# A chunked state-space scan: skip term per head, differences by one-scalar pieces, one exponential per group, the state's decay on two engines

## The reference

```python
acs = jnp.cumsum(dt * A, axis=2)                       # per chunk, always <= 0 and falling
seg = acs[:, :, :, None] - acs[:, :, None, :]
Lmat = jnp.exp(jnp.where(causal, seg, -jnp.inf))
CB = jnp.einsum('bzign,bzjgn->bzijg', Cm, Bm)
M = CB[..., None] * Lmat * dt[:, :, None]
y_diag = jnp.einsum('bzijge,bzjgep->bzigep', M, x)
xw = x * (jnp.exp(acs[:, :, -1:] - acs) * dt)[..., None]
states = jnp.einsum('bzjgn,bzjgep->bzgepn', Bm, xw)
h = h * exp(acs[:, :, -1]) + states                    # from chunk to chunk
y_off = jnp.einsum('bzign,bzgepn->bzigep', Cm, h_prev) * jnp.exp(acs)[..., None]
y = y_diag + y_off + d_skip * x                        # then * silu(z), grouped RMSNorm
```

## Time and profile before

| | |
|---|---|
| median of three runs | 3669.22 us |
| the profiled execution: its time, its span | 3663.91 us, 3661.7 us |
| instructions | 56375 |
| PE busy | 3489.8 us (95%) |
| DVE, POOL, ACT busy | 2014.9, 1576.9, 764.0 us |
| granted PE clock, mean | 0.966 |

### The profile page before, as it was taken

How to read it: one execution, slowest core, us unless ns; L and a number is a source line. 1 busy time by engine, 2 the same in 40 slices (tenths; PEclk the granted TensorE clock), 3 DMA queues, 4 the chain that set the end, 5 groups by cost and what they waited for, 6 DMA issues and landing times.

```text
span 3661.7 us, 56375 instructions
## 1 busy us (share of the span) xinstructions
PE 3489.8 (95%) x22350; PEld 3271.4 (89%) x22350; DVE 2014.9 (55%) x2954; ACT 764.0 (21%) x1537; POOL 1576.9 (43%) x679
## 2 busy tenths in 40 slices
PE   7999999998999999999788889999999899999998
PEld 6999999988977999999667657779999899999998
DVE  5333333346666999987756636866273534334334
ACT  2000000012232111233665425651100200000000
POOL 3533433432322444444357417984443253353351
PEclk9999999999998999999799977999999999999999
DMA  2111111112211222232253326844151111111111
GB/s 85 56 46 34 53 50 34 52 40 76 56 29 58 92 91 91 79 98 92 67 53 105 106 67 176 233 119 150 49 172 50 29 58 40 40 57 40 40 57 52
DMA packets 399841, 272.29 MB, mean 74 GB/s; under 512 B 61843, under 2 KB 375523, under 8 KB 399721
## 3 DMA queue, kind: packets, MB, share of 16 engines
q1 hardware_dynamic: 379896, 225.75, 22.9%
q10 hardware_dynamic: 19824, 44.95, 3.3%
HBM read 211.05 MB, written 59.81 MB: 74 GB/s over the span
## 4 chain that ended last, share of the span: by engine, by line
PE 76%; DVE 15%; issue 3%; POOL 2%; ACT 1%; DMA 1%; another core or an unknown queue 0%; ACTq 0%; SPq 0%; DVEq 0%; POOLq 0%
PE setA L353 8%; PE setA L354 8%; PE setA L355 8%; PE setB L353 8%; PE setB L354 8%; PE setB L355 8%; DVE sc L1095 5%; DVE top L1093 5%; PE bankC L353 2%; PE bankC L355 2%; PE bankC L354 2%; PE bankD L355 2%; PE bankD L353 2%; PE bankD L354 2%; PE bankD L2054 1%
## 5 line engine op out<-in xcount | busy, mean ns | idle before, releaser
L345 POOL TENSOR_TENSOR whi<-wraw,ones 128x1024 fp32r<-128x1024 f32 x192 | 479.0, 2495 | 1669.6 <-PE setA L355 1095.3
L353 PE MATMUL setA<-hhi,whi 128*128 128x352 f32 (+1 forms) x2304 | 755.7, 328 | 40.0 <-POOL wlo L348 12.5
L353 PE MATMUL setB<-hhi,whi 128*128 128x352 f32 (+1 forms) x2304 | 750.0, 326 | 13.6 <-POOL wlo L348 13.6
L354 PE MATMUL setA<-hlo,whi 128*128 128x352 f32 (+1 forms) x2304 | 748.3, 325 | 0.0
L355 PE MATMUL setA<-hhi,wlo 128*128 128x352 f32 (+1 forms) x2304 | 747.1, 324 | 0.0
L354 PE MATMUL setB<-hlo,whi 128*128 128x352 f32 (+1 forms) x2304 | 745.3, 324 | 0.0
L355 PE MATMUL setB<-hhi,wlo 128*128 128x352 f32 (+1 forms) x2304 | 744.2, 323 | 0.0
L348 POOL TENSOR_TENSOR wlo<-wraw,whi 128x1024 fp32r<-128x1024 f32 x192 | 481.7, 2509 | 15.0
L353 PEld LDWEIGHTS setA<-hhi,whi 128*128 128x128 f32 x2304 | 438.6, 190 | 48.8 <-issue 30.6
L353 PEld LDWEIGHTS setB<-hhi,whi 128*128 128x128 f32 x2304 | 436.1, 189 | 18.2 <-POOL wlo L348 14.7
L354 PEld LDWEIGHTS setA<-hlo,whi 128*128 128x128 f32 x2304 | 438.5, 190 | 2.0
(11 more groups left out here) (413 smaller groups left out, 5503.8 us busy)
## 6 DMA issues: line engine op xcount, KB each, us to landing
wraw<-in_w_in SPq DMA_DIRECT2D x64, 512.0 KB, 3.7
wraw<-in_w_ffn_gate SPq DMA_DIRECT2D x44, 512.0 KB, 3.8
wraw<-in_w_ffn_up SPq DMA_DIRECT2D x44, 512.0 KB, 3.8
wraw<-in_w_ffn_down SPq DMA_DIRECT2D x44, 512.0 KB, 3.5
abc<-acsD SPq DMA_DIRECT2D x8, 2048.0 KB, 9.7
xcD<-cv ACTq DMA_DIRECT2D x24, 520.0 KB, 2.7
xc<-xcD SPq DMA_DIRECT2D x8, 1536.0 KB, 14.4
zD<-spill ACTq DMA_DIRECT2D x16, 524.0 KB, 2.7
```

Source lines behind the costliest of these rows:

```text
L345: pool.tensor_tensor(dst_cols(slot, hi), dst_cols(slot), ones[:, :].unsqueeze(1).to_broadcast([P, KD, P]), ALU.mult).then_inc(w_hi, 1)
L353: pe.matmul(out, w1, r1, start=start, stop=False)
L354: pe.matmul(out, w1, r2, start=False, stop=False)
```

## The change

- The skip matmul is made for each head (64 columns of `diag`) where there was one for two heads.
- The differences are made by eight DVE instructions, one for each head, each with two per-partition scalars: minimum with the column's sum, then plus its negative. The exponential needs no bias, and is one activation of 1024 columns.
- ACT copies B to `btok` (`btok_ready`), DVE no longer does.
- The state's decay: POOL takes the first four heads of a group (HPOOL), ACT the other four, one activation each (`ha_done`); ACT's `decay(u)` stands behind `square(u-1)` and waits for `y_done` of u.
- SP's loads and stores are cut into pieces of a group and started group by group; `abc` is loaded once its last readers are done. A few semaphores of the attention part are shared so that two are free.

```diff
+                for g in range(SG):
+                    if nxt is not None and g == 2:
+                        sp.wait_ge(ce_exp, c * SG + SG)
+                        sp.wait_ge(seg_ready, c * SG + SG)
+                        load_acs(nxt, slot)
+                    sp.wait_ge(y2_ready, c * SG + (g + 1))
+                    if nxt is not None:
+                        if g == SG - 1:
+                            load_tok(nxt, slot)
+                            load_rows(nxt, slot, NXB, 2 * SG)
+                        load_rows(nxt, slot, GB * g, GB)
+                    store_rows(c, slot, g)
...
             load_in(0, 0)
             phase_over(sp, 0)
             load_tok(0, 0)
-            load_z(0, 0)
             load_in(1, 1)
             load_tok(1, 1)
-            load_z(1, 1)
+            for slot in range(2):
+                for g in range(SG):
+                    load_z(slot, slot, g)
...
                 wait_u(pe, xdt_ready, c, g, 1)
+                wait_u(pe, btok_ready, c, g, 1)
...
-                        if e % 2 == 0:
-                            pe.matmul(SETS[s][:, 0, m * P:m * P + w], diag[:, GB * g + m, :], xc[slot][:, GB * g + m, 0:w],
-                                      start=True, stop=False)
-                        out = SETS[s][(e % 2) * HD:(e % 2 + 1) * HD, 0, m * P:m * P + w]
+                        hs = slice((e % 2) * HD, (e % 2 + 1) * HD)
+                        out = SETS[s][hs, 0, m * P:m * P + w]
+                        pe.matmul(out, diag[:, GB * g + m, hs], xc[slot][:, GB * g + m, 0:w], start=True, stop=False)
...
-                for e in range(HG):
-                    h = 2 * SH + HG * g + e
-                    ins = act.activation(es[0:w, s, e, 0:w], es[0:w, s, e, 0:w], ACT.Exp, bias=tc[0:w, slot, h:h + 1])
-                ins.then_inc(seg_exp, 1)
+                act.activation(es[0:w, s, :, 0:w], es[0:w, s, :, 0:w], ACT.Exp).then_inc(seg_exp, 1)
+                wait_u(act, xdt_ready, c, g, 0)
+                act.activation(btok[0:w, s, :], bankC[0:w, P:2 * P], ACT.Identity).then_inc(btok_ready, 1)
...
+            def decay(c, g, slot):
+                wait_u(act, y_done, c, g, 0)
...
+                for e in range(HPOOL, HG):
+                    hs = slice(g * GW + e * HD, g * GW + (e + 1) * HD)
+                    ins = act.activation(hT[:, hs], hT[:, hs], ACT.Identity, scale=cd[:, slot, HG * g + e:HG * g + e + 1])
+                ins.then_inc(ha_done, 1)
...
                     wait_u(pool, y_done, c, g, 0)
-                    pool.tensor_tensor(hh_, hh_, cd[:, slot, HG * g:HG * g + HG].unsqueeze(2).to_broadcast([P, HG, HD]),
-                                       ALU.mult).then_inc(hc_done, 1)
+                    pool.tensor_tensor(hh_, hh_, cd[:, slot, HG * g:HG * g + HPOOL].unsqueeze(2)
+                                       .to_broadcast([P, HPOOL, HD]), ALU.mult).then_inc(hc_done, 1)
...
-                v.tensor_tensor(es[0:w, s, :, 0:w], abc[slot][0:w, hs, 0:w],
-                                tc[0:w, slot, SH + HG * g:SH + HG * g + HG].unsqueeze(2).to_broadcast([w, HG, w]), ALU.min)\
-                    .then_inc(seg_ready, 1)
+                for e in range(HG):
+                    h = HG * g + e
+                    ins = v.tensor_scalar(es[0:w, s, e, 0:w], abc[slot][0:w, h, 0:w], tc[0:w, slot, SH + h:SH + h + 1],
+                                          tc[0:w, slot, 2 * SH + h:2 * SH + h + 1], ALU.min, ALU.add)
+                ins.then_inc(seg_ready, 1)
...
-                v.tensor_copy(btok[0:w, s, :], bankC[0:w, P:2 * P])
...
             def state(c, g):
                 wait_u(v, st_done, c, g, 0)
                 wait_u(v, hc_done, c, g, 0)
+                wait_u(v, ha_done, c, g, 0)
```

More of the change, by code:

```diff
@@ L1227, in build @@
         s_kT, s_kTe = sem("smp_kT"), sem("smp_kT_evac")
-        s_sc, s_exp, s_pT, s_pTe, s_zero = (sem(n) for n in ("smp_scores", "smp_exp", "smp_pT", "smp_pT_evac", "smp_zeroed"))
+        s_sc, s_pT, s_pTe = (sem(n) for n in ("smp_scores", "smp_pT", "smp_pT_evac"))
         tail_done, tail_evac, tail_saved = sem("tail_done"), sem("tail_evac"), sem("tail_saved")
@@ L1922, in build @@
          hc_done, h_added, y2_ready, ysq_ready, ssq_done, ssq_copied, small_ready, small_exp, root_done,
-         rstd_ready, rss_in) = (sem("ssd_" + n) for n in (
+         rstd_ready) = (sem("ssd_" + n) for n in (
              "front", "seg", "seg_exp", "ce_exp", "ce", "xdt", "m", "xw", "y", "state", "h_decayed", "h_added",
-             "y2", "ysq", "ssq", "ssq_copied", "small", "small_exp", "root", "rstd", "sample_sums"))
-        Y_OUT0 = [SSD_OUT1 + 16 * (NCH // 2 + 1 + NXB // 4), SSD_OUT1 + 16 * (NCH // 2)]
+             "y2", "ysq", "ssq", "ssq_copied", "small", "small_exp", "root", "rstd"))
+        Y_OUT0 = [SSD_OUT1 + 64 * (NCH // 2 + 1) + 16 * (NXB // 4), SSD_OUT1 + 64 * (NCH // 2)]
+        btok_ready, ha_done = sem("ssd_btok"), sem("ssd_h_decayed_act")
         fin_done, fin_evac = sem("state_T"), sem("state_T_evac")
+        HPOOL = HG // 2
         def over_chunks(eng, step):
@@ L1972, in load_tok, with load_in, load_z @@
                 sp.dma_start(tc[0:w, slot, :], tokD[bass.ds(o, w), :]).then_inc(chunk_loaded[slot], 16)
-            def load_z(c, slot):
+            def load_in(c, slot):
+                load_acs(c, slot)
+                load_rows(c, slot, NXB, 2 * SG)
+                for g in range(SG):
+                    load_rows(c, slot, GB * g, GB)
+            def load_z(c, slot, g):
                 o, w = tok0(c)
-                sp.dma_start(zc[:, slot, :, 0:w], zD.rearrange("(b p) t -> p b t", p=P)[:, :, bass.ds(o, w)])\
+                bs = slice(GB * g, GB * g + GB)
+                sp.dma_start(zc[:, slot, bs, 0:w], zD.rearrange("(b p) t -> p b t", p=P)[:, bs, bass.ds(o, w)])\
@@ L1977, in load_z, with store_rows @@
                     .then_inc(z_loaded[slot], 16)
-            def store_rows(c, slot):
+            def store_rows(c, slot, g):
                 o, w = tok0(c)
-                sp.dma_start(sD.rearrange("(b p) t -> p b t", p=P)[:, :, bass.ds(o, w)], zc[:, slot, :, 0:w])\
+                bs = slice(GB * g, GB * g + GB)
+                sp.dma_start(sD.rearrange("(b p) t -> p b t", p=P)[:, bs, bass.ds(o, w)], zc[:, slot, bs, 0:w])\
                     .then_inc(slot_out[slot], 16)
             def turn(c, slot, used, nxt):
[L1986 to L1990, removed]
+                for g in range(SG):
[10 more added lines that the diff above has]
+                    store_rows(c, slot, g)
@@ L1991, in turn @@
                 if nxt is not None:
                     sp.wait_ge(ysq_ready, c * SG + SG)
-                    sp.wait_ge(slot_out[slot], used * 16 + (SSD_OUT1 + 16))
-                    load_z(nxt, slot)
+                    sp.wait_ge(slot_out[slot], used * 64 + (SSD_OUT1 + 64))
+                    for g in range(SG):
+                        load_z(nxt, slot, g)
             sp.wait_ge(s_sc, 2 * NS)
@@ L2083, in step @@
                     wait_u(pe, xw_ready, c, g, 0)
+                    wait_u(pe, btok_ready, c, g, 0)
                     wait_u(pe, h_added, c, g, 2)
@@ L2156, in step @@
                         square(*one, slot if g >= 1 else 1 - slot)
+                    decay(c, g, slot)
                     if n is not None and nxt is None and g >= 1:
@@ L2164, in part_high @@
                 act.activation(hhi[:, :, o:o + w], qT[:, :, o:o + w], ACT.Identity).then_inc(part_hi, 1)
-            act.activation(sums[:, :, L:T], rss[:, :, :], ACT.Identity).then_inc(rss_in, 1)
+            act.activation(sums[:, :, L:T], rss[:, :, :], ACT.Identity).then_inc(root_done, 1)
             exps(0, 0, 0, 0)
```

44 lines of the change are left out of this document (24 added, 20 removed).

## The result

The changed kernel takes 3713.3 us (median of 4 runs, 3698.5 to 3716.1) against 3667.8 of the kernel before on the same chip: ratio 1.0119 (95% interval 1.0101 to 1.0138), 44 us slower (37 to 51). A second set of 5 runs on another chip gave 1.0108 (1.0092 to 1.0124), 40 us. The forecast was 3692 us, +24, with a range up to 3712, whose end the median passes by 1 us: the direction and the mechanism came true, the size was too small. The profiled execution took 3698.5 us, span 3696.3.

What follows compares the result with a forecast made beforehand. The prediction took PE (6.57 us a unit) and, close behind, the turns of DVE and POOL (6.45) as bounds. Steady units +27, start -6, late `z` +1 and end +2 gave +24: 3692 us, range 3636 to 3712.

Steps and rivals of the forecast that it cites:

- What bounds the kernel: Steady scan: PE sets the 6.57 us unit; SBUF instructions of DVE and POOL exclude each other, turns summing to 6.45 us.
- Part 1: Skip matmul per head avoids PE's switches between column widths; PE's unit falls by about 1.1 us, to 5.5.
- heads one after another: Rival on PE: heads' matmuls run serially, 5.1 us against 3.95, giving 3714 us; within a rival of 10%.
- Part 2: Eight DVE differences at 0.23 us each take 1.84 us, 0.6 more than now, and take turns with POOL.
- Part 3: ACT's work per unit stays 4.2 us, so it has room, but the decay stands ahead of the next `ce`.
- Part 4: On POOL and DVE, `ce` gets in between the fifth and sixth differences; gate to gate takes 7.47 us.
- The sum of turns: DVE's and POOL's mutually exclusive instructions in the changed unit add up to 6.66 us (6.4 to 6.9).
- Part 5: Spread loads remove token waits that cost PE nothing: no gain; the first `z` comes up to 1 us later.
- The sum: Whole kernel: units 5 to 35 +27 us, start -6, late `z` +1, end +2, together +24.
- turns only: Rival: DVE and POOL exclude each other but the differences stay uncut; 6.4 to 6.9 us a unit, 3659 to 3675, 20%.
- Gain cashed: Rival: differences end ahead of `ce`, PE's gain is kept; 5.5 to 6.2 us a unit, 3630 to 3652, 25%.
- PE gets longer: Rival: heads' matmuls run serially, or PE's clock falls from idling (+18 us for five units); 3700 to 3760, 10%.

Runs made afterwards that it cites:

- one_difference_pool_decay: one_difference with POOL doing the whole decay of the state again and ACT none: 3675.0 us.
- one_difference: Changed kernel with its differences as before, one DVE instruction of 1024 columns and eight biased exponentials on ACT: 3658.7 us against 3669.2 for the kernel before.
- ce_eighth: Changed kernel in which POOL multiplies only one of the eight heads of `ce`, the other seven left out: 3653.0 us.
- three_pool_heads: one_difference with the 128-column skip kept in chunk 0's short units and POOL decaying three heads, ACT five: 3650.9 us against 3667.4 for the kernel before.
- ce_first: Changed kernel with ACT making `ce` of the next unit but one ahead of its half of the decay: 3713.9 us.
- ce_after_pieces: Changed kernel in which POOL's multiplication of `ce` also waits for its unit's differences: 3684.5 us against 3672.6 for the kernel before.
- skip_alone: Kernel before with only the skip matmul made per head, 64 columns: no time difference that can be told, unit 6.46 us.
- pieces_alone: Kernel before with only the eight two-scalar differences on DVE and the single exponential on ACT: 3721 us, 49 us slower.
- loads_alone: Kernel before with only the changed kernel's loads and stores, computing as before: ratio 1.0008.

## Why the prediction was right, and where its sizes were off

- *What bounds the kernel*: right. PE at 6.57 us and the turns at 6.45. Without the pieces and with PE quicker the turns showed as 6.3 us (one_difference_pool_decay), 5.9 (one_difference, with the decay shared), and went under PE's 5.76 with three heads on POOL.
- *Part 1*: right in full units, where the output is 3.01 us for a forecast 2.8. PE's unit is 5.76, not 5.5 (ce_eighth, three_pool_heads). **Wrong in the short units**: I gave them 0 to 1 us of gain each. They lose 1.8 to 2 us. The rival "heads one after another" held there and nowhere else. I had read the side-by-side run off full units and carried it over to units of 16 rows without looking at one of theirs.
- *Part 2*: the pieces do take turns with POOL. Their step is 0.256 us, the upper end of 0.20 to 0.26, where I took 0.23: 0.2 us a unit.
- *Part 3*: right, ACT has room (99.8 of 190 us busy). That the decay ahead of `ce` mattered was wrong: ce_first moved it for nothing.
- *Part 4*: the cut is shown. `ce` holds one piece for 2.04 us (2.38 less the 0.334 of an undisturbed one), the fourth instead of the sixth. The loop came to 7.47 us in the forecast and 7.52 in the trace: gate's end to `ce` 2.65 (3.0), `ce` 2.37, the pieces behind it 1.03 (0.69), the rest 1.47. But my reading of it as a latency, in which an earlier `ce` would help, found no support: in ce_first `ce` came 0.45 us sooner and the unit stayed. It is DVE's queue, always full: 8 x 0.256 + 2.04 behind `ce` + 0.30 behind `hT` + 3.13 for the rest = 7.52. That the forecast comes within 0.05 us of it is luck: the pieces are 0.2 us longer than I took, the differences start 0.2 us later behind `hT`, and the hold is 0.3 us shorter than `ce`'s full 2.33, since the caught piece's own 0.3 us pass inside it. What helps is `ce` running beside PSUM instructions (ce_after_pieces, -0.9 us a unit), no `ce` (-1.85) or no pieces (-1.8).
- *The sum of turns* (6.66 us for `ce` running beside PSUM reads): ce_after_pieces has 6.70.
- *Part 5*: "nothing" holds for the loads alone. Beside a quicker PE it does not: the wait for tokens then stops PE (skip_alone).
- *The sum*: 30 units by +0.98 are +29.4 (forecast +27 for 31). The tail +2.5 (+2), but not for the reason given, DVE's longer queue: from the last state to 2450 us pieces_alone has -0.5, skip_alone +2.9 and ce_first, with both, +0.2. What sets it stays open, and the agreement is luck. The start +4.3 instead of -5: this is the mis-sized term, 9 us of the 12 between forecast (+24) and the scan's +36.2. The four short units are +8.5 (forecast -4), the two full ones at the low clock -4.2 (-2 for the one counted there). Of the first short unit's +2.9 the skip explains 1.8 (skip_alone) and the pieces about 1.3 (pieces_alone). The late `z` (+1) shows nowhere: loads_alone has +0.2 over the whole scan.
- Between the scan's +36 us and the +44 and +40 of the medians lie 4 to 8 us. The lower ends of their intervals (+37, +34) come down to about the scan's, so there may be nothing in it; if there is, its cause stays open.
- *Rivals*: "turns only" is what ce_after_pieces is, 6.70 us, within its 6.4 to 6.9. "Gain cashed" would have needed a `ce` that doesn't meet the pieces (ce_eighth). The other half of "PE gets longer" did happen, once: the clock fell under 1.00 within the stretch that I had named as a sign of being wrong. From 2250 to 2257 us PE had been busy 5.08 of 7.00 us at 1.00; then it was granted 0.66, a mean of the two levels 1.2 and 2.4 GHz (columns as in the earlier trace rows):
```profile
2257.00:2262.00 5.00, 5.00 (x48) 4.75 (x48) 5.00 (x8) 1.97 (x6) 3.97 (x2) 0.66 0.95 271
```
From 2262 to 2466 us it was 1.00 again. The fall cost nothing that shows, since DVE set the pace: the units around it took 7.29, 9.57, 5.96 and 7.41 us, 30.2 together, and the next four 30.5.
- *Slips in the working*: 3669.2 + 24 is 3693, not 3692. "Turns only" puts three quarters of its 20% within 0.2%, so the chances should have been 15% for that and 55% for slower, not 10 and 60. A piece's columns at 0.54 ns are 69 ns, not 67. In the earlier trace rows PE's 2.39 busy us and the clock of 0.56 are of the same 5 us, the one does not follow the other.

## What to carry to other kernels

When an instruction is cut into pieces that read and write SBUF on DVE, ask what on POOL may get in between them. The piece that is caught pays for POOL's whole instruction, and a dependence that is free on paper (let POOL's long one wait until the pieces are through) can be worth more than a shorter instruction. Put POOL's long instructions beside DVE's PSUM reads. And take a reading from every form of a unit, the short ones too, before it is multiplied by their number.

## What the runs showed of the hardware

- A `TENSOR_SCALAR` of 128 x 128 f32 on DVE follows the one before after 0.256 us with two per-partition scalars (0.334 long) and is 0.275 long with one.
- PE runs the passes of two heads' 128 x 64 matmuls alternately at 0.054 us a pass, but 128 x 64 and 16 x 64 block by block, 0.325 us a block at 1.2 GHz.
- A piece that POOL's `ce` (2.37 us) gets in ahead of lasts 2.38 to 2.52 us, and of the eight pieces of a unit it is always one (23 of 184 in the changed kernel).
- POOL's decay of 256 columns takes 0.61 us where nothing holds it (ce_after_pieces, at 2357.22) and 1.72 behind DVE's weights, of 512 columns 1.04 and 2.08.
